# A 96-byte gap in front of the arena of a one-core decoder trunk

## The reference, cut to what matters

```python
def trunk(x, start_pos, pool_bufs, conv_bufs, ffn_bufs, p):
    for layer in range(2):
        h = rmsnorm(x, p["mix_norm"][layer])
        if layer % 2 == 0:
            proj = h @ p["w_in_ab"][0]                       # 1024 -> 1536
            ya = multi_scale_pool(...); yb = silu(layernorm(causal_dwconv(a * sigmoid(gt), ...)))
            x = x + concatenate([ya, yb]) @ p["w_out_ab"][0]
        else:
            proj = h @ p["w_in_c"][0]                        # 1024 -> 2048
            z = spatial_gating(layernorm(proj[..., 1024:]), ...)
            x = x + (proj[..., :1024] * z) @ p["w_out_c"][0]
        h = rmsnorm(x, p["ffn_norm"][layer])
        c = causal_dwconv(h @ p["w_up"][layer], ...)         # 1024 -> 5632, 3 taps
        x = x + (silu(c[..., :2816]) * c[..., 2816:]) @ p["w_down"][layer]
    return rmsnorm(x, p["final_norm"]), ...
```

## Time and profile before

| what | value |
|---|---|
| three runs, median | 1164.0 us (1163.71 to 1164.05) |
| the profiled execution: its own time, its span | 1163.62 us, 1161.9 us |
| PE busy | 1145.3 us, 99% of the span |
| DVE, POOL, ACT busy | 818.0, 722.1, 580.0 us |
| granted TensorE clock, mean | 0.998 of full speed |
| DMA | 104.01 MB, 90 GB/s over the span |

### The profile page before, as it was taken

One profiled execution on the slowest core, in us unless ns is written; L12 is line 12 of the kernel. 1 busy time (PEld: TensorE's weight loads), 2 busy tenths in 40 slices (PEclk: granted clock), 3 DMA queues, 4 the chain that ended last, 5 costly groups with the idle time before them and its releaser, 6 DMA issues. The chain is left out here.

```text
span 1161.9 us, 21843 instructions
## 1 busy us (share of the span) xinstructions
PE 1145.3 (99%) x8442; PEld 1124.9 (97%) x8442; DVE 818.0 (70%) x1506; ACT 580.0 (50%) x1113; POOL 722.1 (62%) x691
## 2 busy tenths in 40 slices
PE   8999999999999999999999999999999999999997
PEld 8887999999999999999999999999999999999997
DVE  5999768878677867775614644388686778678655
ACT  7475555544554555453613533366346545654543
POOL 3996344359867985872564324334698679768633
PEclk9999999999999999999999999999999999999999
DMA  6311242203421422131422222322042213232312
GB/s 233 117 56 36 67 146 81 93 28 95 142 65 44 149 73 92 56 137 51 149 84 91 69 69 74 117 82 65 28 147 91 80 61 116 74 92 80 120 51 82
DMA packets 35688, 104.01 MB, mean 90 GB/s; under 512 B 5105, under 2 KB 7153, under 8 KB 35569
## 3 DMA queue, kind: packets, MB, share of 16 engines
q1 hardware_dynamic: 31504, 98.92, 26.9%
q10 hardware_dynamic: 4080, 3.69, 1.1%
HBM read 98.29 MB, written 4.79 MB: 89 GB/s over the span
## 5 line engine op out<-in xcount | busy, mean ns | idle before, releaser
L594 PE MATMUL psum<-x_hi,w_hi 128*128 128x320 f32 (+2 forms) x1564 | 336.4, 297 | 1.3 <-POOL w_lo L1664 1.3
L594 PE MATMUL psum<-x_lo,w_hi 128*128 128x320 f32 (+2 forms) x1564 | 334.8, 295 | 0.0
L594 PE MATMUL psum<-x_hi,w_lo 128*128 128x320 f32 (+2 forms) x1564 | 334.1, 295 | 0.0
L1664 POOL TENSOR_TENSOR w_lo<-w_raw,w_hi 128x1024 fp32r<-128x1024 f32 (+1 forms) x84 | 181.8, 2169 | 188.0 <-ACT w_hi L1041 188.0
L594 PEld LDWEIGHTS psum<-x_hi,w_hi 128*128 128x128 f32 x1564 | 258.8, 188 | 3.6 <-POOL w_lo L1664 1.6
L594 PEld LDWEIGHTS psum<-x_hi,w_lo 128*128 128x128 f32 x1564 | 258.5, 188 | 0.0
L594 PEld LDWEIGHTS psum<-x_lo,w_hi 128*128 128x128 f32 x1564 | 257.3, 188 | 0.0
L2412 DVE SCALAR_TENSOR_TENSOR psum<-arena,params,psum 128x608 f32<-128x608 f32 x176 | 150.4, 854 | 58.8 <-ACT psum L1420 55.8
L1806 POOL TENSOR_TENSOR w_lo<-arena,w_hi 128x384 fp32r<-128x384 f32 x120 | 130.8, 1109 | 49.6 <-ACT w_hi L1331 49.6
L839 PE MATMUL psum<-block_hi,w_lo 128*128 128x288 f32 x504 | 149.2, 296 | 0.0
L839 PE MATMUL psum<-block_hi,w_hi 128*128 128x288 f32 x504 | 149.2, 296 | 0.0
(11 more groups left out here) (270 smaller groups left out, 2207.1 us busy)
## 6 DMA issues: line engine op xcount, KB each, us to landing
w_raw<-in_w_up SPq DMA_DIRECT2D x44, 512.0 KB, 3.7
arena<-in_w_up SPq DMA_DIRECT2D x44, 512.0 KB, 4.3
arena<-in_w_down SPq DMA_DIRECT2D x24, 384.0 KB, 3.6
w_raw<-in_w_down SPq DMA_DIRECT2D x24, 384.0 KB, 3.2
w_raw<-in_w_in_c SPq DMA_DIRECT2D x16, 512.0 KB, 3.5
w_raw<-in_w_in_ab SPq DMA_DIRECT2D x11, 512.0 KB, 3.6
w_raw<-in_w_out_ab SPq DMA_DIRECT2D x16, 256.0 KB, 2.7
w_raw<-in_w_out_c SPq DMA_DIRECT2D x8, 512.0 KB, 3.6
```

The costliest lines, as they stand in the source:

```text
L594: last = nc.tensor.matmul(PS[:, 2 * (q % 2 if slot is None else slot) + half, 0:b - a], w[q][:, k * P:(k + 1) * P], r[:, r_at, a:b], start ...
L1664: nc.gpsimd.tensor_tensor(w_lo[slot][:, 0:nk * P], raws[RAW_SLOT[RAW[u]]][:, 0:nk * P], w_hi[slot][:, 0:nk * P].bitcast(F32), ALU.subtract ...
```

## The change

A filler tile is allocated between `count_corr` and the arena, just large enough that the arena begins at a multiple of 128 bytes, and `at`, from which the hand-placed names count, is taken again behind it.

```diff
         ARENA = 18788
         HIDDEN = 2 * KD * T
         at = -(-nc.sbuf_base // 32) * 32
+        sb("gap", [P, (P - at % P) // 4])
+        at = -(-nc.sbuf_base // 32) * 32
         whole = sb("arena", [P, 2 * HIDDEN + ARENA])
```

## The result

The changed kernel takes 1165.82 us (1165.49 to 1166.31, 20 runs), the kernel before 1163.92 us (1163.54 to 1165.92, 20 runs). The ratio is 1.0015 with a 95% interval of 1.0009 to 1.0021: 1.9 us slower, a difference that is small, clear of the noise, and of the sign that I had not forecast.

A forecast was written before the change was run, and what follows sets the result against it. PE bounds the kernel, by the number of matmuls times their step. All parts of the change summed to zero, so 1163.6 us plus 0, plus 0.4 for the median, gave 1164.0 us, range 1155 to 1173.

The forecast's parts named there:

- I take it, and with it zero for this part: Moving operand of all 8136 float32r matmuls: extra read as a per-matmul cost whatever the address, so the move costs 0.
- PE is the bound and only its step can matter: Whole kernel: PE covers 1145.3 of 1161.9 us, so only the matmul step, or few microseconds at the ends, can matter.
- The 13 ns: Float32r matmuls of 288 columns, L839: the step of 133.1 ns has 13.1 ns over one column a clock.
- aligned fetching: All float32r matmuls: aligned 128-byte pieces are fetched faster, 86.6 us less, 1077 us; chance 0.13, half the gain 0.05.
- clocks of the weight load: Float32r matmuls: loading the next 128 weights takes clocks from the 4-byte stream, an instance offered for the 13 ns.
- needs no address: Float32r matmuls: the per-matmul cost fits all rows without any address, so the moving operand's place was put at zero.
- the 0.7 ns between L870 and L839: Block products: equal 288-column matmuls at different addresses step 133.8 and 133.1 ns; used among the nearest rows for a bound.
- The bound of 1 ns either way, 8.1 us: All 8136 float32r matmuls: the move changes each by 1 ns at most either way, 8.1 us in all.
- Rival C: All float32r matmuls: weights and moving operand, both at multiples of 128, collide more; up to 8.1 us slower, 1167 to 1173; chance 0.18.
- The weights' place in L995: 96 matmuls of L995: weights from `x_hi` or `w_hi` step 120 or 119 ns; 0.1 us at most, taken as nothing.

The follow-up runs named there:

- a gap of 64: Kernel before with the arena moved up by 64 bytes, a distance of 224 from the weights taken at 256: 1168.65 us beside 1163.88.

## Why the prediction was wrong

The step that failed is the one put as "I take it, and with it zero for this part": the moving operand's place was costed at nothing. It costs +2.3 ns on each cut pair (+2.2 in the chain's piece) and gives 0.4 ns (L839) to 1.1 ns (L870, 0.09 us over 84 steps) on each block product, +2.0 us in the span. What decides is the moving operand's distance from the weights: moving both leaves the time as it was (1163.84 us), moving either to the same distance gives the same time (1157.10 and 1157.32). That the change came out at 1.9 us and no more is in part luck, since the kinds of matmul went different ways. Point by point:

- *PE is the bound and only its step can matter.* Right: PE's waits are the same, and the pieces of the chain account for the difference.
- *The 13 ns are a cost of each matmul in this format, and aligned fetching is not it.* Right: 131.4 to 133.3 ns over eight starts, 131.7 and 133.1 at the two that are multiples of 128, and 122.3 ns in bfloat16. The instance that I named, clocks of the weight load, is not proven: the extra falls from 12.9 to 10.0 ns when the weights shrink to a quarter, and not by three quarters.
- *Reading it so "needs no address", hence zero.* This does not follow. A cost that comes with two reads going on at once can hang on how they stand to each other, and it does: 1157.1 to 1168.7 us over eight places. The prediction had a row that spoke against zero: the 0.7 ns between L870 and L839, which it called a difference with addresses, used as a bound and did not cost. At a distance of 64 it is gone (132.3 and 132.2 ns).
- *The bound of 1 ns either way, 8.1 us.* It held as a bound on the time: all eight places lie between 1163.9 − 6.8 and 1163.9 + 4.8. It did not hold for each kind: the two matmuls of a cut pair, allowed 2 ns together, take 2.3 ns more with the change and 3.4 ns more with a gap of 64.
- *Rival C, both reads at multiples of 128.* That the two reads' distance decides is what the runs show; that standing in step is the bad distance is not: the changed kernel's block products, which it would have had slower too, became faster, and a distance of 96 is slower still (1166.4 and 1168.7 us). It was given 0.18 with 1167 to 1173; the effect is a quarter of its price, since the kinds of matmul go different ways.
- *The weights' place in L995 shows no difference that matters.* That row was the evidence at hand. There the distance goes from 32 to 0 at 128; the table has 33.54 and 33.45 for that, 0.4 ns a step. The row, read to 10 ns over five and ten steps, could not show it.

What stays open is what in TensorE or SBUF makes the step hang on the distance, whether its period is 128 or 256 bytes or neither, why 64 and 96 are the best and the worst of the places tried, and why cut pieces fall into different rhythms in two executions of one kernel. No run here looks inside.

## What to carry to other kernels

Alignment by itself was no goal here; the distance between the two operands of a matmul was. Where TensorE is busy all the time with float32r, a sweep of one operand's base over 256 bytes in steps of 32 costs eight runs and was worth 0.5% here. And a trace in which every operand begins at the same place says nothing of another place: bound the cost by the spread between equal matmuls, and don't take zero because the cause that one has in mind needs no address.

## What the runs showed of the hardware that I had not expected

- A step of a float32r matmul is 10 ns longer than that of a bfloat16 one of the same 288 columns (132.3 and 122.3 ns), and hardly shrinks with the weights (130.0 ns with 32 columns).
- Moving the weights and the small tiles by 96 bytes, with the arena kept in place taken at 256, changed a 1164 us kernel by 6.6 us (1163.9 to 1157.3, one execution), without an instruction more or less.
- Four starts 32 bytes apart make no difference to the nanosecond in bfloat16, and up to 1.6 ns a step in float32r.
- The chain's pieces of L839 repeat to 0.01 us within one execution (33.45, 33.44 and 33.44 in the changed kernel's, the three that the chain shows whole), and so are a finer gauge than the time of the whole. The last piece of cut pairs is not: 37.46 and 38.01 us in two executions of one kernel.
